# Order of the down-projection products: W11 of a round ahead of W22 of the round in front of it

## The chip, the cores and the metric

One Trainium2 chip, one core. The metric is the device time of one execution in microseconds (us), as the median of the runs.

## The reference

A trunk of two layers over x of 512 tokens by 1024 features, in float32. Layer 0 mixes the tokens with sliding-window attention, layer 1 with gated linear attention; both are followed by the same feed-forward part, and only that part is touched here:

```python
def conv_ffn(h, w_up, conv_w, conv_b, w_down):
    u = h @ w_up
    gate, up = u[..., :D_FF], u[..., D_FF:]
    gp = jnp.pad(gate, ((0, 0), (CONV_W - 1, 0), (0, 0)))
    conv = conv_b + conv_w[0] * gp[:, 0:S]
    for i in range(1, CONV_W):
        conv = conv + conv_w[i] * gp[:, i:i + S]
    return (jax.nn.silu(conv) * up) @ w_down
    ...
        x = x + conv_ffn(rmsnorm(x, ffn_norm[i]), f_w_up[i], f_conv_w[i], f_conv_b[i], f_w_down[i])
```

D_FF is 2816, and w_down is 2816 by 1024.

## The kernel before

Every float32 product is made of three products of rounded parts: high by high, low by high, high by low. ACT rounds a weight tile to its high part, DVE subtracts to get the low part, and PE multiplies three times per block of 128 rows.

**Phases.** The feed-forward part of a layer is cut along D_FF into two chunks, of 12 and 10 feature tiles. Each chunk has an up phase and then a down phase (`down_phase`), so there are four down phases in the program, called first to fourth here: the first and third work on chunk 0, with 6 pairs of feature tiles (18 matmuls in a product), the second and fourth on chunk 1, with 5 pairs (15 matmuls).

**Rounds.** A down phase has four rounds, one for each two output tiles of 128 features. The two by two blocks (pairs of feature tiles, pairs of output tiles, halves of the tokens) are multiplied in Winograd's form, with seven products in place of eight: Z1, W11, W12, Z2, Z4, Z3 and W22. The W products take plain weight quarters; the Z products take sums of quarters. n is the number of a round over the whole program, r its number in the phase, from 0 to 3; "round two" below is r = 1, "round three" r = 2, "round four" r = 3.

**PE.** `down_product` (L536) waits for the low part of the product's weights, and multiplies into one PSUM bank. There are two sets of three banks (`SETS`), used in turn by rounds. Within a round W11, Z2, Z3 and W22 share one bank: W11 is written, *taken* (added to X by DVE, straight from the bank), Z2 is accumulated on top, taken, then Z3, taken, then W22, taken. So w22(n) waits until Z3 of round n has been taken (L586). w11(n) waits for the taking of W22 two rounds before (L561). The program order of products is `down_phase` (L589 to 611); W22 of a round is multiplied in the round behind it, second in that round's row. The same order stands in the table `ROUNDS` (L73), from which `COUNT` makes the values to wait for.

**DVE.** `down_rounds` (L1564) is its order: takings (`take`, L1484, 128x256), low parts (`weight_lo`, L1456), and the sums of quarters for Z2 and Z4 (`sum_z2` L1465, `sum_z4` L1476). sum_z2 needs W11's quarter, W11's and W12's come by DMA.

**ACT.** `down_round` (L1062) is its order: high parts (`weight_hi`, L1016) of Z3, then of the next round's Z1, this round's W22, the next round's W11, Z2, W12 and Z4. In the second and fourth phase X is final behind each round, so ACT also makes the two tiles that a round has finished: `x_tile` (L968 the scaled and rounded X for the next layer, in the second phase alone; L969 the square). The first of the two waits for the taking of Z4 of the round before, and the second for that of W22 of the round before.

**SP.** `load_round` (L373) issues the loads: W22 of round n when PE is done with W22 of round n-1 (same buffer), W11 and W12 of round n+1 when PE is done with those of round n. In round two it also issues the two first halves of the Z sums of round four (`load_21`), behind the W22 load.

**POOL.** It adds the second halves of those sums by accumulating DMAs (L1962), and in the second and fourth phase it adds the squares of the X tiles one by one into SS (`sum_square`, L1948 and L1951, 128x512). Its order there is: square 0, second half of Z1, square 1, second half of Z3, squares 2 to 5.

Of the kernel before, what the change touches and what calls it, by code (L numbers as in the profile page):

```python
# [70 lines left out]

PRODUCTS = ("Z1", "W11", "W12", "Z2", "Z4", "Z3", "W22")
ROUNDS = ((("Z1", 0), ("W11", 0), ("W12", 0), ("Z2", 0), ("Z4", 0), ("Z3", 0)),  # L73
# [3 lines left out]
COUNT = {(4 * chunk + n, name): 28 * chunk + i + 1  # L77
         for chunk in range(4) for i, (name, n) in enumerate(sum(ROUNDS, ()))}
# [16 lines left out]
def trunk(nc, xT, gains, w_qkv, sinks, rel_bias, w_o, w_bin, w_ga, w_gate, b_norm, w_bo, w_up, conv_w, conv_b,  # L95
          w_down0, w_down1, onehot, ident, causal, causal_pair, out, bias_rows):
    with ExitStack() as ctx:
# [227 lines left out]
        def _(sp):  # L325
# [20 lines left out]
            def load_down(n, name):  # L346

                sp.dma_start(DRAW[name][:, 0:down_cols(n)], quarter(n, name)).then_inc(plain[name], 16)
# [24 lines left out]
            def load_round(n, src, next_unit):  # L373

                r = n % 4
                if r:
                    sp.wait_ge(down_done, COUNT[n - 1, "W22"])
                    load_down(n, "W22")
                if r == 1:
                    layer, chunk = n // 8, n // 4 % 2  # L380
                    sp.wait_ge(al_last, 2 * layer + chunk + 1)
                    load_21(n + 2, "Z1")
                    load_21(n + 2, "Z3")
                if r < 3:
                    sp.wait_ge(down_done, COUNT[n, "W11"])
                    load_down(n + 1, "W11")
                    sp.wait_ge(down_done, COUNT[n, "W12"])
                    load_down(n + 1, "W12")
                if src is not None and r == 2:
                    sp.wait_ge(down_lo["Z3"], n)  # L390
                    load(next_unit, src[0])
                    sp.wait_ge(down_lo["Z3"], n + 1)
                    load(next_unit + 1, src[1])
# [79 lines left out]
        def _(pe):  # L473
# [76 lines left out]
            def z1(n, ready=None):  # L550
                if n % 4 == 0:
                    pe.wait_ge(unit_done, chunk_end(n))
                if n % 4 == 1:
                    pe.wait_ge(value_ready, gated_end(n) - 1)
                if n % 4 >= 2:
                    pe.wait_ge(x_taken, COUNT[n - 2, "Z4"])
                down_product(n, "Z1", SETS[n % 2][2], True, ready)

            def w11(n, ready=None):
                if n % 4 >= 2:  # L560
                    pe.wait_ge(x_taken, COUNT[n - 2, "W22"])  # L561
                down_product(n, "W11", SETS[n % 2][0], True, ready)
# [22 lines left out]
            def w22(n):  # L585
                pe.wait_ge(x_taken, COUNT[n, "Z3"])  # L586
                down_product(n, "W22", SETS[n % 2][0], False)

            def down_phase(layer, chunk):  # L589
                n = 8 * layer + 4 * chunk  # L590
                parts = AL_LAYER * layer + AL_COUNT[chunk]
                z1(n, lambda kb: parts + 2 * kb + 1)
                w11(n)
                w12(n, lambda kb: parts + 2 * kb + 2)
                z2(n, lambda kb: parts + 2 * kb + 2 + (kb == PAIRS[chunk] - 1))
                z4(n)
                z3(n)
                for m in (n + 1, n + 2):
                    z1(m)
                    w22(m - 1)  # L600
                    w11(m)
                    w12(m)
                    z2(m)
                    z4(m)
                    z3(m)
                w11(n + 3)
                w22(n + 2)
                z1(n + 3)
                z2(n + 3)
                z4(n + 3)  # L610
                z3(n + 3)
                w12(n + 3)
# [726 lines left out]
        def _(dve):  # L1339
# [148 lines left out]
            def take_w11(n):  # L1488
                take(n, "W11", 0, 0, t1, ALU.add)
# [16 lines left out]
            def take_w22(n):  # L1506
                take(n, "W22", 0, 1, t1, ALU.subtract)
# [56 lines left out]
            def down_rounds(n, st, next_unit):  # L1564

                take_z1(n)
                last_lo(n // 8, n // 4 % 2, PAIRS[n // 4 % 2] - 1, 5, 7)
                weight_lo(n, "Z4")
                weight_lo(n, "Z3")
                take_w12(n)  # L1570
                take_z2(n)
                sum_z2(n + 1)
                weight_lo(n + 1, "Z1")
                take_z4(n)
                weight_lo(n, "W22")
                weight_lo(n + 1, "W11")
                sum_z4(n + 1)
                for m in (n + 1, n + 2):
                    take_z3(m - 1)
                    weight_lo(m, "W12")  # L1580
                    weight_lo(m, "Z2")
                    take_z1(m)
                    weight_lo(m, "Z4")
                    take_w22(m - 1)
                    weight_lo(m, "Z3")
                    take_w11(m)
                    take_w12(m)
                    weight_lo(m, "W22")
                    take_z2(m)
                    sum_z2(m + 1)  # L1590
                    if m == n + 1:
                        weight_lo(m + 1, "Z1")
                        take_z4(m)
                        sum_z4(m + 1)
                        weight_lo(m + 1, "W11")
                    else:
                        weight_lo(m + 1, "W11")
                        take_z4(m)
                        sum_z4(m + 1)
                        weight_lo(m + 1, "Z1")  # L1600
                m = n + 3
                take_z3(m - 1)
                weight_lo(m, "Z2")
                take_w11(m)
                weight_lo(m, "Z4")
                take_w22(m - 1)
                weight_lo(m, "W12")
                weight_lo(m, "Z3")
                if st is not None:
                    x_lo(st, 0)  # L1610
                take_z1(m)
                if st is not None:
                    x_lo(st, 1)
                    x_lo(st, 2)
                take_z2(m)
                weight_lo(m, "W22")
                if st is not None:
                    x_lo(st, 3)
                take_z4(m)
                if next_unit is not None:  # L1620
                    lo_unit(next_unit)
                if st is not None:
                    x_lo(st, 4)
                take_z3(m)
                if st is not None:
                    x_lo(st, 5)
                if next_unit is not None:
                    lo_unit(next_unit + 1)
# [513 lines left out]
```

## Time and profile before

| what | value |
|---|---|
| time, median of 3 runs | 1089.37 us (1086.51 to 1090.02) |
| time of the profiled execution | 1087.98 us |
| its span, first to last instruction | 1086.2 us |
| mean granted TensorE clock | 0.996 |
| PE busy | 1072.6 us, 99% |
| DVE busy | 752.9 us, 69% |
| ACT busy | 493.5 us, 45% |
| POOL busy | 117.3 us, 11% |
| DMA, mean rate | 112 GB/s |

Busy time is the time in which the profiler shows an instruction on an engine. PE's matmuls overlap in the record, so a busy PE can still have small delays between the starts of its matmuls; these are found from the number of matmuls in a stretch and the stretch's length. PEld is the weight load of PE, which runs ahead of its matmul.

### The profile page before, as it was taken

What the parts mean: (1) busy time and instruction counts of PE and PEld (TensorE: products, weight loads), DVE (VectorE), ACT (ScalarE), POOL (GpSimd) and SP (SyncE); (2) the same over time, 40 slices, a digit from 0 to 9 for tenths busy, and PEclk for the clock granted to TensorE, in tenths of its full rate; (3) what the DMA queues carried; (4) which work ended last, traced back from release to release, by engine and by line L of the source; (5) the groups of instructions that cost most, each with busy time, mean ns of one, the idle gap of its engine ahead of it and who ended that gap; (6) DMA issues with size and microseconds to landing.
All of it is one profiled execution on the core that took longest, in us unless ns stands there. A gap on an engine that the chain in (4) does not pass through costs nothing.

```text
span 1086.2 us, 15688 instructions
## 1 busy us (share of the span) xinstructions
PE 1072.6 (99%) x5920; PEld 921.5 (85%) x5920; DVE 752.9 (69%) x1098; ACT 493.5 (45%) x766; POOL 117.3 (11%) x109
## 2 busy tenths in 40 slices
PE   9999999999999999999999999999999999999996
PEld 7888788888899888898888888788888899888896
DVE  6588667676876667787544566867676876667786
ACT  7366554343533334454652335454344432344452
POOL 3100030000100000123021221130000100000122
PEclk9999999999999999999999999999999999999998
DMA  7511032225652225552222211232226652225542
GB/s 211 168 59 59 27 110 97 97 97 183 161 161 98 96 95 170 135 161 71 78 78 97 78 44 56 72 108 92 96 96 184 159 172 87 97 97 169 133 122 91
DMA packets 43804, 121.12 MB, mean 112 GB/s; under 512 B 5250, under 2 KB 10530, under 8 KB 43748
## 3 DMA queue, kind: packets, MB, share of 16 engines
q1 hardware_dynamic: 36308, 106.81, 28.9%
q0 software_dynamic: 4608, 11.54, 6.5%
q10 hardware_dynamic: 2832, 2.01, 1.1%
q8 instruction: 37, 0.61, 0.2%
q14 instruction: 19, 0.16, 0.0%
HBM read 116.93 MB, written 2.88 MB: 110 GB/s over the span
## 4 chain that ended last, share of the span: by engine, by line
PE 94%; DVE 3%; ACT 1%; DMA 1%; issue 0%; SPq 0%; DVEq 0%
PE PS L486 68%; PE PS L544 19%; PE PS L666 1%; PE PS L684 1%; PE PS L674 1%; DVE XL L1368 1%; DMA X<-xT 1%; PE PS L816 1%; DVE X L1916 1%; PE PS L848 0%; PE PS L835 0%; PE PS L819 0%; PE PS L850 0%; PE PS L745 0%; PE PS L772 0%
## 5 line engine op out<-in xcount | busy, mean ns | idle before, releaser
L486 PE MATMUL PS<-XH,WH 128*128 128x512 f32 x992 | 391.4, 395 | 1.0 <-DVE WL L1663 1.0
L486 PE MATMUL PS<-XH,WL 128*128 128x512 f32 x992 | 386.4, 389 | 0.0
L486 PE MATMUL PS<-XL,WH 128*128 128x512 f32 x992 | 386.1, 389 | 0.0
L486 PEld LDWEIGHTS PS<-XH,WH 128*128 128x128 f32 x992 | 186.2, 188 | 42.1 <-issue 2.1
L486 PEld LDWEIGHTS PS<-XH,WL 128*128 128x128 f32 x992 | 186.2, 188 | 39.4
L486 PEld LDWEIGHTS PS<-XL,WH 128*128 128x128 f32 x992 | 186.3, 188 | 38.4 <-issue 1.0
L939 ACT CAST WH<-WRAW 128x1024 fp32r<-128x1024 f32 x134 | 139.5, 1045 | 161.1 <-DMA WRAW<-w_up 110.3
L1351 DVE TENSOR_TENSOR WL<-WRAW,WH 128x1024 fp32r<-128x1024 f32 x134 | 168.6, 1258 | 16.2 <-ACT WH L939 15.7
L1389 DVE TENSOR_TENSOR GS<-PS,R 128x512 f32<-128x512 f32 x44 | 30.4, 692 | 118.8 <-PE PS L486 118.8
L544 PE MATMUL PS<-AH,DH_Z 128*128 128x256 f32 x352 | 98.2, 279 | 0.3
L544 PE MATMUL PS<-AH,DL_Z 128*128 128x256 f32 x352 | 97.6, 277 | 0.0
L544 PE MATMUL PS<-AL,DH_Z 128*128 128x256 f32 x352 | 97.6, 277 | 0.0
L982 ACT ACTIVATE CV<-GS,CONVB,CONVW 128x512 f32<-128x512 f32 x44 | 36.0, 819 | 89.0 <-DVE GS L1389 89.0
L544 PE MATMUL PS<-AH,DH_W 128*128 128x256 f32 x264 | 73.7, 279 | 0.2 <-DVE X L1484 0.2
L544 PE MATMUL PS<-AL,DH_W 128*128 128x256 f32 x264 | 73.2, 277 | 0.0
L544 PE MATMUL PS<-AH,DL_W 128*128 128x256 f32 x264 | 73.2, 277 | 0.0
L1484 DVE TENSOR_TENSOR X<-X,PS 128x256 f32<-128x256 f32 x112 | 46.1, 417 | 38.1 <-PE PS L544 37.7
L544 PEld LDWEIGHTS PS<-AH,DH_Z 128*128 128x128 f32 x352 | 66.4, 189 | 2.3 <-PE PS L486 1.9
L544 PEld LDWEIGHTS PS<-AL,DH_Z 128*128 128x128 f32 x352 | 66.1, 188 | 0.0
L544 PEld LDWEIGHTS PS<-AH,DL_Z 128*128 128x128 f32 x352 | 66.1, 188 | 0.0
L1016 ACT CAST DH_W<-DRAW_W 128x768 fp32r<-128x768 f32 (+1 forms) x48 | 37.0, 780 | 53.8 <-DMA DRAW_W<-w_down 53.7
L544 PEld LDWEIGHTS PS<-AH,DH_W 128*128 128x128 f32 x264 | 49.9, 189 | 0.6 <-DVE X L1484 0.6
(234 smaller groups left out, 1514.5 us busy)
## 6 DMA issues: line engine op xcount, KB each, us to landing
WRAW<-w_up SPq DMA_DIRECT2D x88, 512.0 KB, 3.3
WRAW<-w_bin SPq DMA_DIRECT2D x24, 512.0 KB, 3.3
DRAW_W<-w_down SPq DMA_DIRECT2D x24, 384.0 KB, 3.8
DRAW_W<-w_down SPq DMA_DIRECT2D x24, 320.0 KB, 3.0
WSUM_Z<-w_down SPq DMA_DIRECT2D x12, 384.0 KB, 4.8
WSUM_Z<-w_down POOLq DMA_DIRECT2D x12, 384.0 KB, 6.3
WRAW<-w_qkv SPq DMA_DIRECT2D x8, 512.0 KB, 3.4
WSUM_Z<-w_down SPq DMA_DIRECT2D x12, 320.0 KB, 3.8
```

What stands on the lines that cost most here:

```text
L486: last = mm(PS[:, bank], w[:, c:c + P], x[:, kb], start=start and n == 0 and w is wh and x is hi, stop=stop and n == len(kbs) - 1 and w is wl)
L544: last = mm(PS[:, bank, 0:TH], w[:, c], act_part[:, kb, x], start=start and kb == 0 and w is DH[name] and act_part is AH, stop=kb == PAIRS ...
L666: last = mm(PS[:, B4 + k % 2, c:c + P], q, keys[:, first:first + P], start=True, stop=True)
L674: last = nc.tensor.transpose(PS[:, B6, i * P:(i + 1) * P], PB[:, k % 2, i], IDENT[:])
L684: last = mm(PS[64 * half:64 * half + 64, B7, j * P:(j + 1) * P], V[:, 1 - j if p else 0, p, g * HD:(g + 1) * HD], PT[:, k % 2, 2 * j + hal ...
L816: mm(PS[:, B4, c], EN[:, h, c], EP[:, h, c], start=True, stop=True)
L939: nc.scalar.copy(WH[s][:], WRAW[s][:]).then_inc(hi_ready, 1)
L982: A(CV[:, par], GS[:, par, 2:T + 2], ACT.Identity, bias=CONVB[:, layer, tile], scale=CONVW[:, layer, tile, 2]).then_inc(c0_ready, 1)
L1016: nc.scalar.copy(DH[name][:, c], raw[:, c]).then_inc(down_hi[name], 1)
L1351: tt(WL[s][:], WRAW[s][:], WH[s][:].bitcast(F32), ALU.subtract).then_inc(lo_ready, 1)
L1389: tt(GS[:, par, 2:T + 2], PS[:, 2 * par], R[:], ALU.mult).then_inc(unit_evac, 2)
L1484: tt(x, x, PS[:, SETS[n % 2][bank], 0:TH], op).then_inc(x_taken, 1)
```

## The change

In rounds two and three of each down phase, W11 of the round is multiplied ahead of W22 of the round before. The takings on DVE follow this order, and so do the waits and loads on SP: in these rounds the wait for W11 and the load of the next W11 stand first, then the wait for W22 and its load, then the two `load_21` of round two, then W12. Nothing is added or taken away. ACT and POOL keep their orders.

```diff
@@ ROUNDS
-          (("Z1", 1), ("W22", 0), ("W11", 1), ("W12", 1), ("Z2", 1), ("Z4", 1), ("Z3", 1)),
-          (("Z1", 2), ("W22", 1), ("W11", 2), ("W12", 2), ("Z2", 2), ("Z4", 2), ("Z3", 2)),
+          (("Z1", 1), ("W11", 1), ("W22", 0), ("W12", 1), ("Z2", 1), ("Z4", 1), ("Z3", 1)),
+          (("Z1", 2), ("W11", 2), ("W22", 1), ("W12", 2), ("Z2", 2), ("Z4", 2), ("Z3", 2)),
@@ load_round (SP)
                 r = n % 4
+                if r in (1, 2):
+                    sp.wait_ge(down_done, COUNT[n, "W11"])
+                    load_down(n + 1, "W11")
                 if r:
                     sp.wait_ge(down_done, COUNT[n - 1, "W22"])
                     load_down(n, "W22")
...
-                if r < 3:
+                if r == 0:
                     sp.wait_ge(down_done, COUNT[n, "W11"])
                     load_down(n + 1, "W11")
+                if r < 3:
                     sp.wait_ge(down_done, COUNT[n, "W12"])
                     load_down(n + 1, "W12")
@@ down_phase (PE)
                     z1(m)
+                    w11(m)
                     w22(m - 1)
-                    w11(m)
                     w12(m)
@@ down_rounds (DVE)
                     take_z1(m)
                     weight_lo(m, "Z4")
+                    take_w11(m)
+                    weight_lo(m, "Z3")
                     take_w22(m - 1)
-                    weight_lo(m, "Z3")
-                    take_w11(m)
                     take_w12(m)
```

On PE, at the start of round two of the first phase (the names end in the product: DH_ and DL_ are the high and low parts of its weights), before:

```order
L544 MATMUL PS<-AH_117,DH_Z1_72 128x256
L544 MATMUL PS<-AL_118,DH_Z1_72 128x256
L544 MATMUL PS<-AH_117,DL_Z1_73 128x256
L544 MATMUL PS<-AH_117,DH_W22_69 128x256
L544 MATMUL PS<-AL_118,DH_W22_69 128x256
L544 MATMUL PS<-AH_117,DL_W22_70 128x256
```

and now:

```order
L548 MATMUL PS<-AH_117,DH_Z1_72 128x256
L548 MATMUL PS<-AL_118,DH_Z1_72 128x256
L548 MATMUL PS<-AH_117,DL_Z1_73 128x256
L548 MATMUL PS<-AH_117,DH_W11_75 128x256
L548 MATMUL PS<-AL_118,DH_W11_75 128x256
L548 MATMUL PS<-AH_117,DL_W11_76 128x256
```

Behind Z1 now comes W11, and W22 follows where W11 stood.

On SP, the loads of rounds two and three of the first phase (DRAW_ is the buffer that a quarter lands in, WSUM_Z13 and WSUM_Z33 those of `load_21`; the name in brackets is the semaphore waited for), before:

```order
L348 DMA DRAW_W22_71<-w_down0 128x768 [waits down_done]
L352 DMA WSUM_Z13_126<-w_down0 128x768 [waits al_last]
L352 DMA WSUM_Z33_125<-w_down0 128x768
L348 DMA DRAW_W11_77<-w_down0 128x768 [waits down_done]
L348 DMA DRAW_W12_83<-w_down0 128x768 [waits down_done]
L348 DMA DRAW_W22_71<-w_down0 128x768 [waits down_done]
L348 DMA DRAW_W11_77<-w_down0 128x768 [waits down_done]
L348 DMA DRAW_W12_83<-w_down0 128x768 [waits down_done]
```

and now:

```order
L348 DMA DRAW_W11_77<-w_down0 128x768 [waits down_done]
L348 DMA DRAW_W22_71<-w_down0 128x768 [waits down_done]
L352 DMA WSUM_Z13_126<-w_down0 128x768 [waits al_last]
L352 DMA WSUM_Z33_125<-w_down0 128x768
L348 DMA DRAW_W12_83<-w_down0 128x768 [waits down_done]
L348 DMA DRAW_W11_77<-w_down0 128x768 [waits down_done]
L348 DMA DRAW_W22_71<-w_down0 128x768 [waits down_done]
L348 DMA DRAW_W12_83<-w_down0 128x768 [waits down_done]
```

The load of W11 has moved in front of that of W22 and of the two `load_21`. DVE's two takings that change places read alike in such a list (both are X from PS), and the low part of Z3 stays between them.

## Rows read from the trace of the kernel before

**Rows 1.** The page, busy time of each engine over the span.
```profile
PE 1072.6 (99%) x5920; PEld 921.5 (85%) x5920; DVE 752.9 (69%) x1098; ACT 493.5 (45%) x766; POOL 117.3 (11%) x109
```

**Rows 2.** Windows, PE's down matmuls in the four phases: length, busy (count), clock, DMA.
```profile
287.38:344.63 57.25, 57.25 (x504) 1.00 0.47 134
453.66:503.44 49.78, 49.56 (x420) 1.00 0.45 129
856.92:914.16 57.24, 57.24 (x504) 1.00 0.46 133
1023.20:1070.81 47.61, 47.56 (x405) 1.00 0.40 104
```

**Rows 3.** Windows, PE's down matmuls over five products at two places.
```profile
455.49:463.99 8.50, 8.50 (x78) 1.00 0.32 103
...
479.90:488.73 8.83, 8.83 (x78) 1.00 0.68 232
```

**Rows 4.** Timeline, PE's weight loads: start, us, engine, line, operands [idle before <-releaser].
```profile
465.66 0.19 PEld L544 LDWEIGHTS PS<-AH,DH_W 128*128 128x128 f32 x1
...
1047.31 0.19 PEld L544 LDWEIGHTS PS<-AH,DL_Z 128*128 128x128 f32 x1
1047.74 0.19 PEld L544 LDWEIGHTS PS<-AH,DH_W 128*128 128x128 f32 x1 [0.24 <-DVE X L1484]
```

**Rows 5.** Timeline, DVE in the second down phase.
```profile
462.98 1.56 DVE L1456 TENSOR_TENSOR DL_W<-DRAW_W,DH_W 128x640 fp32r<-128x640 f32 x2
...
465.19 0.42 DVE L1484 TENSOR_TENSOR X<-X,PS 128x256 f32<-128x256 f32 x1
...
469.52 0.41 DVE L1484 TENSOR_TENSOR X<-X,PS 128x256 f32<-128x256 f32 x1
...
474.12 0.83 DVE L1465 TENSOR_TENSOR DRAW_Z<-WSUM_Z,DRAW_W 128x640 f32<-128x640 f32 x1 [0.67 <-DMA DRAW_W<-w_down]
...
476.67 0.82 DVE L1456 TENSOR_TENSOR DL_W<-DRAW_W,DH_W 128x640 fp32r<-128x640 f32 x1
...
479.53 1.58 DVE L1456 TENSOR_TENSOR DL_Z<-DRAW_Z,DH_Z 128x640 fp32r<-128x640 f32 x1
...
485.40 0.42 DVE L1484 TENSOR_TENSOR X<-X,PS 128x256 f32<-128x256 f32 x1 [0.55 <-PE PS L544]
```

**Rows 6.** Timeline, ACT in round two of the second phase.
```profile
468.90 0.72 ACT L968 ACTIVATE XH<-X,GAIN 128x512 fp32r<-128x512 f32 x1 [1.10 <-DVE X L1484]
...
470.05 0.71 ACT L1016 CAST DH_Z<-WSUM_Z 128x640 fp32r<-128x640 f32 x1
470.67 0.72 ACT L1016 CAST DH_W<-DRAW_W 128x640 fp32r<-128x640 f32 x1
```

**Rows 7.** Timeline, SP: issue of W22's and the next W11's load, second phase.
```profile
467.72 0.33 SPq L348 DMA_DIRECT2D DRAW_W<-w_down  x1
...
469.49 0.33 SPq L348 DMA_DIRECT2D DRAW_W<-w_down  x1
```

**Rows 8.** DMA issues: W22's load in round two, phases first to fourth; last number: landing.
```profile
DRAW_W<-w_down SPq DMA_DIRECT2D x1, 384.0 KB, 4.2
...
DRAW_W<-w_down SPq DMA_DIRECT2D x1, 320.0 KB, 2.7
...
DRAW_W<-w_down SPq DMA_DIRECT2D x1, 384.0 KB, 3.0
...
DRAW_W<-w_down SPq DMA_DIRECT2D x1, 320.0 KB, 3.2
```

**Rows 9.** Timeline, POOL's additions of squares, rounds two and four of the second phase.
```profile
472.50 1.62 POOL L1951 TENSOR_TENSOR SS<-SS,SQ 128x512 f32<-128x512 f32 x1
...
490.41 1.29 POOL L1951 TENSOR_TENSOR SS<-SS,SQ 128x512 f32<-128x512 f32 x1 [6.24 <-ACT SQ L969]
```

**Rows 10.** Timeline, DVE in round two of the fourth phase.
```profile
1042.96 1.85 DVE L1465 TENSOR_TENSOR DRAW_Z<-WSUM_Z,DRAW_W 128x640 f32<-128x640 f32 x1 [0.22 <-DMA DRAW_W<-w_down]
```

**Rows 11.** Windows, DVE in round four of the second phase.
```profile
492.46:502.25 9.79, 9.79 (x16) 1.00 0.25 85
```

## The prediction

> **What bounds the kernel now.** The page first: PE is busy for 99% of the span [rows 1], so what can be won lies in the small delays between its matmuls. I read those from the windows over PE's matmuls in the four down phases. In the first and third, 504 matmuls take 57.25 and 57.24 us, one every 0.1136 us [rows 2], with no wait that I could find: this is PE's own pace, and nothing can be won there. At this pace the 420 matmuls of the second phase would take 47.71 us and the 405 of the fourth (its last product left out) 46.01; they take 49.78 and 47.61 [rows 2]. **2.07 and 1.60 us, 3.67 together (0.34%), is all that any order of these products can give back.**
>
> Two things make up this loss. One is plain waits. W22's first weight load in round two of the second phase starts at 465.66; it was due about 0.08 earlier, and the taking of Z3 that it needs ended at 465.19 + 0.42 = 465.61 [rows 4, 5]. In round three of the fourth phase the same load starts 0.43 us behind its predecessor in place of 0.12, released by a taking: 0.31 lost [rows 4]. The other is pace: five products (75 matmuls; the windows also count those that reach over an edge) take 8.50 us before the first stall and 8.83 after it, at the same granted clock of 1.00 [rows 3]. So after a stall a matmul starts every 0.1177 us in place of 0.1133, and the trace of the second phase goes on so for some 18 products: 15 x 18 x 0.0044 = 1.2 us.
>
> **The change, part by part**, worked out for the second phase, since its rows are the fullest. A product is 15 x 0.1133 = 1.70 us. Round two's Z1 starts at 463.99 (the end of the first window of [rows 3]) in both kernels.
>
> *W11 moved ahead of W22.* W11 is now due at 463.99 + 1.70 = 465.69. Its low part is ready at 462.98 + 1.56 = 464.54 [rows 5]: no wait. W22 is due at 467.39, and Z3 was taken at 465.61: the wait of 0.08 is gone, and PE keeps its fast pace. In round three W11 comes 1.7 us earlier than now, so its low part is the new thing that can be late (below).
>
> *SP.* A load is issued 0.19 behind its product's end (W22 ends at 467.53, issue at 467.72 [rows 7]). W11's next load goes out at 467.39 + 0.19 = 467.58, and no longer at 469.49 [rows 7]; DVE's sum for Z2, which waited 0.67 us for it [rows 5], finds it landed. W22's load goes from 467.72 to 469.09 + 0.19 = 469.28, and the two load_21 behind it from about 468.1 to 469.7.
>
> *ACT and DVE behind W22's load.* It lands after 2.7 us [rows 8], at 472.0. ACT has by then taken the second X tile (it waits for the taking of W22, which now stands where W11's stood, 469.52 + 0.41 = 469.93 [rows 5]; 1.15 for the tile and 0.62 for Z1's high part [rows 6] make 471.7), so the DMA sets the time: high part 472.0 to 472.8 (0.73), low part to 473.6, then the taking of Z2, 473.55 + 0.42 = 474.0. Z3 is due at 463.99 + 6 x 1.70 = 474.19. So PE isn't held as long as the load lands within 2.9 us; with W22's 18 matmuls and 768 columns the same sum in the first and third phase gives 3.7 us. The rows say 4.2, 2.7, 3.0 and 3.2 for the four phases [rows 8]: **the first exceeds its bound by 0.5, the fourth by 0.3.** sum_z2 starts at 473.9 in place of 474.12 [rows 5]: DVE's late start and the earlier W11 cancel.
>
> *POOL.* Its addition of square 1 stands behind the second half of Z1 that follows load_21. In the trace it runs at 472.50 for 1.62 us [rows 9], when DVE mostly waits. It now comes some 1.6 us later, 474.1 to 475.7, on top of DVE's unbroken run of sum, low part of Z1, taking, sum, low part of W11. What this costs DVE I take from ops that met such an addition: 1.58 us in place of 0.82 [rows 5] and 1.85 in place of 0.83 [rows 10], 0.76 to 1.02; nothing if it meets a wait of DVE. I take 0.76, the second phase's own. Low part of W11, by starts 0.735 apart, a taking 0.335: 473.9 + 0.735 + 0.735 + 0.335 + 0.735 + 0.82 = 477.26, + 0.76 = 478.0. PE wants it at 463.99 + 8 x 1.70 = 477.59. **PE waits 0.4 at W11 of round three**, and the slow pace starts there. At the product behind (W12 of round three, now at 481.66) PE is then at 477.59 + 0.4 + 0.08 + 2 x 1.77 = 481.6. The gain of the first step is given back.
>
> *Round three to the end, second phase.* W22's load moves by 1.7 us again: issued about 481.8, landed 484.6, low part done at 486.2, so Z2's taking starts at 486.2 and no longer at 485.40 [rows 5]: 0.8 late. DVE then works without a gap into round four, where the addition of square 4 (490.41 [rows 9]) comes as much later and holds a low part again. From 492.46 to 502.25 DVE has no idle time at all, 9.79 of 9.79 us busy [rows 11], and PE's last products wait for its takings: the lateness goes through whole. Bounds: 0 (if round three's slack takes it) and 1.7 (the whole shift). I take **+0.9**, near the 0.8 just worked out.
>
> *Fourth phase.* No rounded X tile, so ACT is freer. Z3 of round two waits 0.3 (above), W11 of round three about 0.5, and the old losses there, 0.31 and a stall before it, go: **+0.3**, between -1.6 (its whole loss) and +2.
>
> *First and third.* DVE has gaps there and POOL adds no squares. The third's load lands in time: 0. The first's, if it lands in 4.2 us again, stalls Z3 by 0.5, and the slow pace holds for the 15 products behind, 270 x 0.0044 = 1.2: +1.7. If it lands within 3.7, nothing. I take half, **+0.85**.
>
> A fit in the Trainium skill, "DMA: Bandwidth & Descriptors", in "Anatomy of one DMA" (2.0 us and the bytes over 436 GB/s, made for transfers that GpSimd issues), gives 2.9 us for such a load as an estimate. By it the first phase costs nothing and the sum would be +1.2. The row of 4.2 speaks against it here, that of 3.0 for it.
>
> Sum: +0.9 + 0.3 + 0.85 = +2.05. The profiled execution took 1087.98 us, of which 1086.2 are the span and 1.8 lie around it; it would take 1090.0. It stands 1.39 below the median of 1089.37, so the median becomes **1091.4 us**. A change under 0.3%, 3.3 us, can't be told from none here.
>
> **The rivals.**
> - *The load is hidden everywhere* (all of W22's loads land within their bounds). For it: two of four rows. Then only the second phase's late DVE and a little of the fourth are left: +1.2, 1090.6.
> - *A gain.* POOL's addition falls into a wait of DVE, or DVE's ops keep it out. The Trainium skill, "SBUF — State Buffer", in "SBUF: two separate sides", says that VectorE and GpSimd share a port pair as an exclusive lock, held for a whole instruction by whichever starts first. Ops back to back would then delay POOL and not DVE until a taking lets it in. Then W11's low part is ready at 477.26, before 477.59, PE keeps its pace, and the 1.2 us of slow pace and 0.08 of the second phase and 0.7 of the fourth return: -2.0, 1087.4. Against it: the op of 1.58 us in the same phase, and DVE's full round four. The faster side needs nearly all of the 3.67.
> - *W22's load becomes the bound* (the side of slower). From 2.9 us on in the second and fourth phase, and 3.7 in the first and third, Z3 waits in round two and again in round three. If all land in 4.2 us: 1.3 at the first and about 0.6 at the second, +1.9 in each of second and fourth, +1.7 in each of first and third: +7.2, 1096.6. With landings between, +3.3 to +5. For it: the row of 4.2, and that the load now starts while W11's is still landing.
> - *It doesn't matter* (the new waits are as long as the old): 1089.4.
>
> **How the numbers follow.** Forecast 0.42 (0.02 of it over the bound of slower), hidden load 0.15, gain 0.14 (0.04 of it faster by over 0.3%), W22's load as the bound 0.24, no effect 0.05. So faster 0.04, same 0.70, slower 0.26. The range goes from 1087.8, just above the gain, to 1095.0, which takes in most of the load's case; about 0.1 is left out on each side.
>
> **What would show it.** Right: no wait of PE at W22 in rounds two and three; in the second and fourth phase a wait at W11 of round three released by its low part, or at Z3 by the taking of Z2; W22's load issued some 1.6 us later; POOL's addition of square 1 over a sum or low part of DVE that takes 1.6 us or more; the second phase longer than 49.78 us. Wrong: the second phase at 48.5 us or less, or the first and third both over 58 us (then the load's price was set too low).

## The result, and the profile after

The changed kernel takes 1091.36 us in the median of 11 runs (1090.09 to 1092.12), the kernel before, beside it on the same chip, 1088.4 us in the median of 11 (1086.51 to 1090.02). The ratio is 1.0025, with a 95% interval of 1.0015 to 1.0034: slower by 3.0 us, which is real, and less than 0.3%. The time forecast was 1091.4. That it fits so well is partly luck: the forecast added 2.05 us to a median of three runs, 1089.37, that stood 1.0 us above the median of eleven, and the true step was 2.96.

The profiled execution took 1092.12 us with a span of 1090.2, 4.0 more than before. The page, busy time (before: [rows 1]):

```profile
PE 1071.8 (98%) x5920; PEld 920.0 (84%) x5920; DVE 755.1 (69%) x1098; ACT 492.4 (45%) x766; POOL 117.7 (11%) x109
```

DVE is busy for 2.2 us more, with the same 1098 instructions: something stretches them. The windows over PE's down matmuls in the four phases (length, busy, count, clock, DMA):

```profile
288.26:345.61 57.35, 57.35 (x504) 1.00 0.43 130
454.65:506.34 51.69, 49.22 (x420) 1.00 0.44 126
859.83:917.07 57.24, 57.24 (x504) 1.00 0.44 132
1026.11:1074.80 48.69, 47.42 (x405) 1.00 0.36 98
```

Beside [rows 2]: +0.10, +1.91, 0.00 and +1.08, together 3.09. The clock is the same. The rest of the span's 4.0 is the 0.88 by which the first down phase starts later, ahead of any product that was moved; the medians' difference, 2.96, is near the 3.09 without it. So 2.99 of the loss is in the second and fourth phase. PE's waits (line, releaser: total, times, longest), in 453 to 507 us,

```profile
PE PS L548 <- DVE DL_Z L1460: 1.3, 1, 1.3
PE PS L548 <- DVE X L1488: 1.0, 1, 1.0
```

and in 1026 to 1075 us:

```profile
PE PS L548 <- DVE DL_Z L1460: 1.3, 1, 1.3
```

The first and third of these are one wait: **Z1 of round three, for its low part**. By the starts of the matmuls it costs 1.56 us in the second phase and 1.51 in the fourth (the profile's 1.3 counts only from the modelled end of the matmul before). It was not there before (0.00 and 0.26). The second is Z4 of round four, 1.29, also new. DVE in the second phase, and below it the same sum in the fourth:

```profile
473.91 0.83 DVE L1460 TENSOR_TENSOR DL_W<-DRAW_W,DH_W 128x640 fp32r<-128x640 f32 x1 [1.51 <-ACT DH_W L1020]
474.65 0.42 DVE L1488 TENSOR_TENSOR X<-X,PS 128x256 f32<-128x256 f32 x1
474.98 2.57 DVE L1469 TENSOR_TENSOR DRAW_Z<-WSUM_Z,DRAW_W 128x640 f32<-128x640 f32 x1
477.48 0.81 DVE L1460 TENSOR_TENSOR DL_Z<-WSUM_Z,DH_Z 128x640 fp32r<-128x640 f32 x1
...
496.83 1.78 DVE L1372 SCALAR_TENSOR_TENSOR XL<-X,GAIN,XH 128x512 fp32r<-128x512 f32 x1
...
1046.57 2.51 DVE L1469 TENSOR_TENSOR DRAW_Z<-WSUM_Z,DRAW_W 128x640 f32<-128x640 f32 x1
```

The third row is the sum for Z2, 0.83 us before [rows 5], now 2.57. POOL at the same times:

```profile
474.68 0.86 POOL L1966 DMA_DIRECT2D WSUM_Z<-w_down  x1 [5.84 <-DMA WSUM_Z<-w_down]
475.25 1.61 POOL L1955 TENSOR_TENSOR SS<-SS,SQ 128x512 f32<-128x512 f32 x1
...
496.46 1.60 POOL L1955 TENSOR_TENSOR SS<-SS,SQ 128x512 f32<-128x512 f32 x1 [0.97 <-ACT SQ L973]
...
1046.74 1.64 POOL L1955 TENSOR_TENSOR SS<-SS,SQ 128x512 f32<-128x512 f32 x1
```

POOL's addition ends at 475.25 + 1.61 = 476.86, DVE's sum at 477.55, 0.69 behind it. In the fourth phase 1048.38 and 1049.08: 0.70. The sum is nearly all done after the addition; then comes the low part of Z1 (477.48 to 478.29), and PE takes it up at once (Z1 starts at 478.43; it was due at 476.87). The landings of W22's load in round two (last number), first to fourth phase:

```profile
DRAW_W<-w_down SPq DMA_DIRECT2D x1, 384.0 KB, 3.7
...
DRAW_W<-w_down SPq DMA_DIRECT2D x1, 320.0 KB, 2.9
...
DRAW_W<-w_down SPq DMA_DIRECT2D x1, 384.0 KB, 3.1
...
DRAW_W<-w_down SPq DMA_DIRECT2D x1, 320.0 KB, 3.0
```

The first, second and fourth are on the bound that the prediction set (3.7 and 2.9) within 0.1, the third is 0.6 inside it, and Z3 of round two waits 0.08, 0.06, 0.00 and 0.18 us.

**Theory A**, for the experiments: the load is late by one product (1.7 us), with it the loads of the halves behind it, POOL and DVE's sum; so POOL's addition of square 1 falls on the sum and holds it to its own end. **Theory B**: W22's load is the cost, DVE waits for its high part and everything behind is late. **Theory C**: the new order of the products and takings costs by itself, in either round.

### The profile page after: what moved, and what is told of

Its sections match the earlier page's. It is cut to its first block, busy times and chain, and to the rows that moved or that the text cites. A ratio compares the mean times of both kernels' runs of the same rounds, so it can differ in the third digit from the quotient of the medians.

```text
span 1090.2 us, 15688 instructions
## 1 busy us (share of the span) xinstructions
PE 1071.8 (98%) x5920; PEld 920.0 (84%) x5920; DVE 755.1 (69%) x1098; ACT 492.4 (45%) x766; POOL 117.7 (11%) x109
## 4 chain that ended last, share of the span: by engine, by line
PE 93%; DVE 4%; DMA 1%; ACT 1%; issue 1%; SPq 0%; DVEq 0%
PE PS L490 68%; PE PS L548 18%; PE PS L670 1%; DMA DRAW_W<-w_down 1%; PE PS L688 1%; PE PS L678 1%; DMA X<-xT 1%; DVE XL L1372 1%; PE PS L820 1%; DVE X L1920 1%; PE PS L852 0%; PE PS L839 0%; PE PS L823 0%; PE PS L854 0%; PE PS L749 0%
## 5 line engine op out<-in xcount | busy, mean ns | idle before, releaser
L1460 DVE TENSOR_TENSOR DL_W<-DRAW_W,DH_W 128x768 fp32r<-128x768 f32 (+1 forms) x48 | 42.6, 896 | 12.7 <-ACT DH_W L1020 12.7
```

What stands on the lines that cost most here:

```text
L1460: tt(DL[name][:, c], raw[:, c], DH[name][:, c].bitcast(F32), ALU.subtract).then_inc(down_lo[name], 1)
```

## The experiments

A wait at a product is the extra time before its first and its second matmul together, by starts of matmuls; phase lengths are those of the windows. Experiments 1 to 4 ran on one chip and 5 to 12 on another, each beside the kernel before.

**1 and 2. The swap in one round alone.** Table, product order, takings and loads go back to the order before in the other round. Against the changed kernel, experiment 1 (swap in round two alone) and then 2 (in round three alone):

```diff
-          (("Z1", 2), ("W11", 2), ("W22", 1), ("W12", 2), ("Z2", 2), ("Z4", 2), ("Z3", 2)),
+          (("Z1", 2), ("W22", 1), ("W11", 2), ("W12", 2), ("Z2", 2), ("Z4", 2), ("Z3", 2)),
...
-                if r in (1, 2):
+                if r == 1:
```

```diff
-          (("Z1", 1), ("W11", 1), ("W22", 0), ("W12", 1), ("Z2", 1), ("Z4", 1), ("Z3", 1)),
+          (("Z1", 1), ("W22", 0), ("W11", 1), ("W12", 1), ("Z2", 1), ("Z4", 1), ("Z3", 1)),
...
-                if r in (1, 2):
+                if r == 2:
```

> The change in round two alone; round three as before. Both theories: round two's wait comes back (1.5 us at Z1 of round three in the second and fourth phase), since W22's load of round two is late and the two load_21 with it. If round two carries it all, the second phase is 51 to 52 us and the fourth 48.4 to 48.9; if round three carries half, the second is about 50.7.

> The change in round three alone; round two as before. If round two carries the loss (theory P in its narrow form), the fourth phase stays at 47.6 and the second is at 49.8 to 50.6: what is left is W22's load of round three, issued 1.7 us later, which makes DVE's taking of Z2 some 0.8 us late there. If the lateness of W22's load is what counts, round three loses as much as round two: the second phase is at 50.7 or more.

Round two alone: median 1090.37, ratio 1.0019 (1.0010 to 1.0029); phases 57.25, 51.44, 57.25, 47.94, with Z1 of round three waiting 1.57 and 1.53. Round three alone: 1089.01, ratio 1.0007 (0.9998 to 1.0017); phases 57.25, 50.33, 57.40, 46.52, and Z1 of round three waits 0.25 and 0.00. The long wait belongs to the swap in round two, where the load of the halves and POOL's addition of square 1 stand behind W22's load. Theory C fails for round three: there the swap costs 0.55 in the second phase (Z4 of round four waits 1.05) and gives 1.09 back in the fourth, where no change was expected. Some 0.7 of this 1.09 is pace, since 30 matmuls run at the slow one in place of 194; in experiment 1 too the fourth phase came out shorter than expected, at the fast pace nearly throughout. The waits are the surer reading.

**3 and 4. POOL's addition of square 1 ahead of the second half of Z1**, in the changed kernel and in the kernel before:

```diff
+                    if chunk:
+                        sum_square(st + 1, 1)
                     add_quarter(n + 3, "Z1")
-                    if chunk:
-                        sum_square(st + 1, 1)
                     add_quarter(n + 3, "Z3")
```

> The changed kernel, with POOL's addition of square 1 ahead of the second half of Z1 (in the second and fourth phase). Theory P (the addition of square 1, behind the accumulating DMA, falls on DVE's sum for Z2 and holds it, 2.57 us in place of 0.83): the addition now runs at about 472.7 in the second phase, while DVE waits for W22's high part; the sum takes 0.83 us again, the wait of 1.5 us at Z1 of round three goes from both phases, the second phase takes 50.0 to 50.7 us (51.69 now) and the fourth, without its last product, 47.2 us (48.69); the time is 1088.5. Theory L (W22's load, issued 1.7 us later, is the bound by itself): the sum still ends too late, Z1 of round three still waits for over 1 us, and both phases stay within 0.4 us of 51.69 and 48.69.

> The kernel before, with the same move on POOL. Theory P: the additions no longer meet the sum of the fourth phase (1.85 us there), the waits of 0.3 at Z1 and at W22 of round three go; the fourth phase takes 46.2 to 47.2 us in place of 47.61, the second stays at 49.8 within 0.5; 1087.5 in all. Theory L: nothing changes by more than 0.3 us in either phase.

Changed kernel: 1088.39, ratio to before 1.0001 (0.9992 to 1.0010), phases 57.24, 50.02, 57.24, 46.96. Kernel before: 1088.03, ratio 1.0001 (0.9992 to 1.0010), 57.25, 49.80, 57.25, 47.44. One line moved on POOL takes the loss away, and does not change the time of the kernel before. There its fourth phase had been expected at 47.2 or less: the waits of 0.3 at Z1 and W22 of round three did go, but 299 matmuls ran at the slow pace in place of 194, and took 0.5 back. DVE's sum in the changed kernel with this edit, second phase,

```profile
473.98 0.82 DVE L1469 TENSOR_TENSOR DRAW_Z<-WSUM_Z,DRAW_W 128x640 f32<-128x640 f32 x1
```

and POOL's addition, now in a wait of DVE:

```profile
471.17 1.29 POOL L1955 TENSOR_TENSOR SS<-SS,SQ 128x512 f32<-128x512 f32 x1 [3.50 <-ACT SQ L973]
```

The wait at Z1 of round three is gone in both phases. W22's load is as late as in the changed kernel, so theory B has little left: Z3 of round two waits 0.23 and 0.33.

**5. The changed kernel without W22's loads of rounds two and three.** W22's parts are then made from what lies in its buffer as soon as PE is done with it, so the output is not the reference's. The line that drops the loads:

```diff
-                    load_down(n, "W22")
+                    if r == 3:
+                        load_down(n, "W22")
```

> The changed kernel without W22's loads in rounds two and three: ACT rounds what lies in the buffer as soon as PE is done with it, so the output is another and only the 2.9 us of the transfer are gone from the chain. Theory P+L (W22's late load pushes DVE's sum for Z2 into the time when POOL is about to add square 1): in the second phase ACT is busy until 472.7 of the trace of the change, so W22's low part comes 0.45 us earlier, the sum starts just ahead of POOL's addition and the low part of Z1 behind it is held instead: Z1 of round three still waits 0.3 to 1 us. In the fourth phase, where ACT is free 1.3 us earlier, the sum is done ahead of the addition; the wait at Z1 goes below 0.3 us and the phase, without its last product, takes 46.3 to 47 us (48.69 now). Theory P alone (the addition costs the same wherever the sum starts): both waits at Z1 stay within 0.2 of 1.5 us.

One run, 1091.2; phases 57.24, 51.23, 57.24, 47.84. Z1 of round three still waits, 1.28 and 0.86, and the sum still takes 2.63 us, beside an addition at 475.34. Neither outcome as written: the waits are shorter than 1.5, and the fourth phase isn't near 47. Taking the transfer away gives 0.46 and 0.85 of 1.91 and 1.08. But this edit moves the addition as well. Counted from the starts of the phases (455.11 and 1026.08) it ends 0.37 and 0.84 us earlier than in the changed kernel, and the waits at Z3 and Z1 together are shorter by 0.35 and 0.83. So PE's loss follows the addition's end, and the transfer acts by where it puts the addition.

**6 and 7. POOL's additions cut to 4 of 512 columns in the second and fourth phase, in the changed kernel and in the kernel before**, which leaves out nearly all of these sums of squares:

```diff
+                w = 4 if st in (2, 4) else T
...
-                    nc.gpsimd.tensor_tensor(SS[:], SS[:], SQ[:, par], ALU.add).then_inc(ss_ready, 1)
+                    nc.gpsimd.tensor_tensor(SS[:, 0:w], SS[:, 0:w], SQ[:, par, 0:w], ALU.add).then_inc(ss_ready, 1)
```

> The changed kernel with POOL's additions of the squares made over 4 columns in place of 512 in the second and fourth phase (the sum of squares that the output needs is not computed there). Theory P: no DVE op is held for over 1 us in these phases; the waits at Z1 of round three (1.56 and 1.51) and at Z4 of round four (1.29) fall to under 0.2 each; the second phase takes 48.3 to 49.5 us and the fourth 46.3 to 46.9. Theory L: the late load remains, Z1 of round three waits over 1 us, and the second phase stays above 51 us.

> The kernel before, with the POOL engine's additions of squares cut to 4 of 512 columns in the second and fourth phase (so part of the sums of squares is left out, and the output is not the reference's). The counterpart of e6_small_squares, for what the additions cost before. If the changed kernel was hurt because its order moved the addition onto DVE's sum, the additions cost the kernel before much less than the 3.3 and 1.6 us that they cost the changed one: about 1 us in the second phase (48.8), and 0.3 in the fourth (47.3). If they cost as much here, the collision was there all along and the swap is not what made it matter: 46.5 and 46.

One run each, 1087.7 and 1086.4. The second and fourth phase of the kernel before, without the additions:

```profile
454.08:503.27 49.19, 49.19 (x420) 1.00 0.50 136
1023.02:1069.14 46.12, 46.12 (x405) 1.00 0.40 104
```

The changed kernel has 48.36 and 47.05. The additions thus cost the kernel before 0.6 and 1.5 us, and the changed one 3.3 and 1.6. Over both phases: with additions the change costs 100.38 - 97.39 = 2.99, without them 95.41 - 95.31 = 0.10. **Without the additions the two kernels take the same time in these executions.** This is a balance, though, and not the absence of a cost. The changed order is 0.93 longer in the fourth phase, with Z3 waiting 0.46 and 0.35, and faster by 0.83 in the second, where the kernel before runs 313 matmuls at the slow pace, 1.4 us worth, and the changed one none. With each slow matmul taken off at 0.0044 us, the swap costs 1.5 us over both phases without the additions and 4.2 with them. Nor does the fourth phase split as expected: the additions cost 1.5 us there before (expected 0.3), as much as after. Each is one run; the firmer proof that the additions carry the net loss is experiments 3 and 4, with 11 runs each. DVE and POOL in the changed kernel without additions:

```profile
475.09 0.82 DVE L1469 TENSOR_TENSOR DRAW_Z<-WSUM_Z,DRAW_W 128x640 f32<-128x640 f32 x1
```

```profile
474.88 0.86 POOL L1967 DMA_DIRECT2D WSUM_Z<-w_down  x1 [5.85 <-DMA WSUM_Z<-w_down]
475.45 0.53 POOL L1956 TENSOR_TENSOR SS<-SS,SQ 128x4 f32<-128x4 f32 x1
```

The accumulating DMA's 0.86 us on POOL lies over the sum and does not hold it.

**8. The loads of the halves ahead of W22's load**, so that POOL is as early as before and W22's load meets more traffic:

```diff
-                if r:
-                    sp.wait_ge(down_done, COUNT[n - 1, "W22"])
-                    load_down(n, "W22")
                 if r == 1:
...
                     load_21(n + 2, "Z1")
                     load_21(n + 2, "Z3")
+                if r:
+                    sp.wait_ge(down_done, COUNT[n - 1, "W22"])
+                    load_down(n, "W22")
```

> The changed kernel, with the loads of the two halves of Z1 and Z3 of round four issued ahead of W22's load in round two (they wait for less). The POOL engine's DMA and its addition of square 1 then come about as early as in the kernel before, and W22's load lands later by the bytes ahead of it, 0.5 to 1 us. If the loss comes from the addition meeting DVE's sum for Z2, the wait at Z1 of round three goes down from 1.5 to 0.5 us or less, and the second phase is near 50.5. If the loss comes from W22's load being late, the wait stays at 1.5 us or grows, and PE may wait at Z3 of round two also: 52 us or more.

1093.87, ratio 1.0055 (1.0040 to 1.0071), the slowest of all; phases 58.77, 51.42, 58.27, 47.92. Neither outcome as written: both parts came true. The collision is gone, and the load is late. DVE, second phase:

```profile
476.41 0.83 DVE L1460 TENSOR_TENSOR DL_W<-DRAW_W,DH_W 128x640 fp32r<-128x640 f32 x1 [3.03 <-ACT DH_W L1020]
...
477.48 0.82 DVE L1469 TENSOR_TENSOR DRAW_Z<-WSUM_Z,DRAW_W 128x640 f32<-128x640 f32 x1
```

POOL's addition (474.53 to 476.14) falls into DVE's wait of 3.03 us; the sum takes 0.82, and Z1 of round three doesn't wait. But W22's load, issued at the same point of the phase (15.61 us behind its start, in both kernels), lands after

```profile
DRAW_W<-w_down SPq DMA_DIRECT2D x1, 320.0 KB, 4.4
```

in place of 2.9, and Z3 of round two waits 1.56 us: the excess over the bound of 2.9, 1.5, goes straight to PE. The first and third phase lose 1.52 and 1.01 in the same way; there too the load is issued at the same point as in the changed kernel (18.67 and 18.68 us behind the starts), and lands after

```profile
DRAW_W<-w_down SPq DMA_DIRECT2D x1, 384.0 KB, 5.1
...
DRAW_W<-w_down SPq DMA_DIRECT2D x1, 384.0 KB, 4.6
```

against the bound of 3.7.

**9 and 12. Mending the order.** The changed kernel with POOL's addition first, and with W22's low part moved behind the sum for Z4 (in round two also behind W11's low part), so that DVE doesn't wait for W22's high part ahead of the taking of Z2 (W22 is not needed before two more products, now that W11 stands ahead of it):

```diff
                     take_w12(m)
-                    weight_lo(m, "W22")
                     take_z2(m)
...
                         sum_z4(m + 1)
                         weight_lo(m + 1, "W11")
+                        weight_lo(m, "W22")
...
                         sum_z4(m + 1)
+                        weight_lo(m, "W22")
                         weight_lo(m + 1, "Z1")
```

> The changed kernel with square 1 first on POOL and, on DVE, W22's low part moved behind the next round's W11 (round two) or the sum for Z4 (round three), where nothing waits for it yet. If W22's load acts through DVE's order alone (DVE waits for its high part and the taking of Z2 stands behind it), the waits of PE at Z3 of rounds two and three (0.23 and 0.14 in the second phase, 0.33 in the fourth, of the kernel with square 1 first) go; the second phase falls from 50.02 to about 49.6, the fourth from 46.96 to 46.1 to 46.6. If the load acts otherwise, nothing changes by over 0.2 us.

> The kernel of e9_low_later once more, beside e11_low_later_before on the same chip: 1087.2, phases of 57.2, 49.2, 57.2 and 46.4. If its lead over the kernel before (0.8 us) was chance, it comes out within 0.2 us of it.

1087.21, ratio 0.9990 (0.9981 to 0.9999), then 1087.0, ratio 0.9993 (0.9984 to 1.0002). This is the best version found, 0.8 to 0.9 us under the kernel before in both comparisons: under 0.3%, and at the edge of what its runs can tell from none. The windows of the second execution:

```profile
287.92:345.17 57.25, 57.25 (x504) 1.00 0.48 132
454.20:503.68 49.48, 48.83 (x420) 1.00 0.50 134
857.15:914.40 57.25, 57.25 (x504) 1.00 0.47 133
1023.43:1069.49 46.06, 46.06 (x405) 1.00 0.41 106
```

The fourth phase stands at its floor of 46.01 (in the first execution it was 46.44, with 89 matmuls at the slow pace); what the second still loses lies in round four.

**10. The taking of Z1 ahead of X's first low part in round four**, added to 9, against the wait at Z4 of round four. In the changed kernel that was 1.29 us, behind the X tile (496.83, 1.78 us) that POOL's addition holds; in experiment 9 it had already come down to 0.26:

```diff
+                take_z1(m)
                 if st is not None:
                     x_lo(st, 0)
-                take_z1(m)
-                if st is not None:
                     x_lo(st, 1)
```

> As e9_low_later, and in round four of the second phase DVE takes Z1 ahead of the first low part of the next layer's X, which a POOL addition holds for 1.77 us. The wait of PE at Z4 of round four (1.29) falls to under 0.3 us; DVE has no idle time from there to the phase's end, so W22 of round four may wait longer in turn: the second phase 48.7 to 49.6 us, the fourth as in e9. In all 1086.5 to 1087.5, the first version below the kernel before.

1087.4, ratio 0.9992 (0.9983 to 1.0001); second phase 49.81. Z4 no longer waits, but W22 of round three (in round four) waits 0.60 and Z3 1.01, in place of 0.00 and 0.64 (0.35 and 0.66 in the second execution of that kernel): the lateness moves to the next product. No gain.

**11. The mends of 9 in the kernel before**, where W22's low part stands ahead of W11's, since W22 is multiplied first. Round two's part of the edit, to which POOL's line and round three's are added as in 9:

```diff
+                        weight_lo(m, "W22")
                         weight_lo(m + 1, "W11")
```

> The kernel before with the two mends of e9_low_later: the addition of square 1 ahead of the second half of Z1, and the low part of W22 taken out of its place ahead of the taking of Z2 and put behind the sum for Z4. In this order W22 still comes ahead of W11, so its low part stands ahead of W11's. If what e9 won comes from these mends alone, and the order of W11 and W22 does not matter once they are in, this kernel comes out like e9: second phase 49.2, fourth 46.4, median 1087.2 beside 1088.0 of the kernel before. If W22 behind Z1 is really too early for its parts (the order's own worth), the low part moved back makes the wait at W22 of round three longer than its 0.3, the second phase stays at 49.8 or goes over 50, and the median stays at 1088 or more.

1089.59, ratio 1.0013 (1.0004 to 1.0022), 2.6 us above 12 on the same chip; phases 58.34, 49.49, 57.25, 46.97. In the first phase W22 waits 1.08 us in round three. DVE's sum for Z2 there, in this kernel,

```profile
312.96 0.96 DVE L1465 TENSOR_TENSOR DRAW_Z<-WSUM_Z,DRAW_W 128x768 f32<-128x768 f32 x1 [1.32 <-DMA DRAW_W<-w_down]
```

and in that of 12:

```profile
311.03 0.95 DVE L1469 TENSOR_TENSOR DRAW_Z<-WSUM_Z,DRAW_W 128x768 f32<-128x768 f32 x1
```

From the starts of the phases (288.45 and 287.92) that is 24.5 and 23.1 us. In the old order the sum waits for W11's load, and W22's low part now stands behind it, close to its due time; with W11 multiplied first its load goes out a product earlier and W22 is due a product later. So the later place of W22's low part needs the changed order of products: the first and fourth phase differ by 1.09 and 0.91 us between 11 and 12, the second by 0.01. What 9 gives takes both.

## Why the prediction was right, and where it was not

**The chain up to the collision was right to 0.2 us.** The second phase starts 0.99 us later in the profile after (454.65, before 453.66), so 0.99 is added to the times of the prediction:

| step, second phase | predicted | measured |
|---|---|---|
| W22's load issued | 470.27 | 470.26 |
| it lands | 472.99 | 473.12 |
| taking of Z2 starts | 474.54 | 474.65 |
| sum for Z2 starts | 474.89 | 474.98 |
| POOL's addition of square 1 starts | 475.09 | 475.25 |
| low part of Z1 starts | 475.63 | **477.48** |

**The step that failed is the price of the addition.** "I take 0.76, the second phase's own", from two ops that had met an addition, with 0.76 to 1.02 as bounds. It was 2.57 - 0.82 = 1.75, outside the bounds. The bounds were durations of two encounters, where the two ends should have been compared: in [rows 5] the op of 1.58 us ends at 479.53 + 1.58 = 481.11, and POOL's addition that it met ran 478.75 to 480.44. It too ended 0.67 behind the addition. A held op of DVE ends some 0.7 us behind the addition, so its price is what is left of the addition when it would start, and not a fixed 0.76.

**Which op is held.** The traces have two kinds of meeting, and the forecast took the price of one for the other. In the usual kind the addition comes while DVE is at work on a low part; this one runs on as if alone, and the next is held. DVE and then POOL in the profile after, a little behind the collision:

```profile
481.08 0.81 DVE L1460 TENSOR_TENSOR DL_Z<-DRAW_Z,DH_Z 128x640 fp32r<-128x640 f32 x1
481.81 0.41 DVE L1488 TENSOR_TENSOR X<-X,PS 128x256 f32<-128x256 f32 x1
482.14 1.58 DVE L1460 TENSOR_TENSOR DL_Z<-DRAW_Z,DH_Z 128x640 fp32r<-128x640 f32 x1
```

```profile
481.35 1.68 POOL L1955 TENSOR_TENSOR SS<-SS,SQ 128x512 f32<-128x512 f32 x1 [3.20 <-ACT SQ L973]
```

This costs 0.76 with a taking between the two ops, and 1.09 without (1.91 in place of 0.82, at 1048.34 before and 1052.60 after). In the other kind the op at work is held as well, from its very start: so it went with the sum for Z2, 0.27 and 0.17 us old when the addition started. By the usual kind the sum would have ended at 475.80, the addition 1.15 later and Z1's low part 0.68 behind it, at 477.63 in place of 478.29: a wait of 0.9 at Z1, as an estimate from these rows. The other 0.66 comes from the sum being held.

**So the wait's place was wrong too.** With the 0.76 at the low part of W11 PE was to wait 0.4 there. The 1.75 fell on the sum, one op ahead of Z1's low part, which had 0.2 us to spare: 1.56 at Z1 of round three. The wait at W11 behind it is 0.08.

**The terms.** Second phase +0.9, measured +1.91; fourth +0.3, measured +1.08; first +0.85, measured +0.10; third 0, measured 0. Two terms too small by 1.8 and one too large by 0.75 gave +2.05 for 3.09. The bounds of the fourth, -1.6 to +2, held; those of the second, 0 to 1.7, did not.

**The first phase.** The load landed in 3.7 us and not in 4.2, so half of a 1.7 us loss was not due: 0.08 of waiting, and no slow pace behind it. The bound itself was right; experiment 8 crossed that of 2.9 by 1.5 and PE waited 1.56.

**Pace.** "The slow pace starts there" was wrong for the second phase. PE's matmuls from W22 of round three on, two products behind the long stall, in four products of the second phase and five of the fourth:

```profile
482.04:488.84 6.80, 6.80 (x62) 1.00 0.64 207
```

```profile
1053.60:1062.43 8.83, 8.83 (x77) 1.00 0.35 111
```

6.80 is 4 x 1.70, the fast pace, and 8.83 is the slow one of [rows 3]. In the second phase 18 matmuls ran at the slow pace after the change and 271 before, so 253 x 0.0044 = 1.1 us were won back there by pace; without this the phase would have cost 3.0. The prediction had counted this gain as given back at W11.

**The two waits removed** (W22 in rounds two and three) are gone, as forecast. **Late DVE into round four** was there, but as a new wait at Z4 (1.29): X's low part took 1.78 us, held by square 5's addition, ending at 498.61 behind POOL's 498.06, with the taking of Z1 behind it. That POOL's ops come later and hold an op again was in the prediction; only its size was not.

**The rivals.** *W22's load as the bound* did not happen here (0.00 to 0.18 us of waiting), but was near: experiment 8 made it so, 1093.87. *A gain* was to come if the addition fell into a wait of DVE: experiments 3 and 9 put it there, and their medians are 3.0 and 4.2 us under that of the change. Against the kernel before that is no difference and 0.8 us, not the 2.0 of this rival. As for the rule named with it (the Trainium skill, "SBUF — State Buffer", "SBUF: two separate sides"), by which whoever starts first holds the lock for a whole instruction: the traces agree that a whole instruction is waited out, and mostly on who waits. In the second and fourth phase, over the twelve traces with whole additions, a low part (of a weight or of X) was at work 56 times when an addition started, and took 0.74 to 0.82 us each time, as if alone; the addition ended 1.14 us or more behind it. In six more meetings the sum for Z2 was the older by 0.17 to 0.43 us and was held all the same (the profile after and experiments 1 and 5, two each). In these six the addition stands right behind POOL's own DMA, whose record (0.86 to 0.88 us) reaches 0.3 into that of the addition. Why they differ stays open: in experiment 6 the same DMA and an addition of 4 columns did not hold the sum, and POOL's starts are rough.

## What to carry over

When an instruction moves, find what moves with it on queues behind it (here a load took two other loads and so POOL's DMA and addition along), and ask what each of them now lies on top of. An op of VectorE that an addition of GpSimd holds costs what is left of that addition, so read such a price from the two ends, not from the op's length; look which of two neighbouring ops is the held one, and put the addition where VectorE waits anyway. And when a product is made due later, its preparation has to be moved back as well, or it holds up what has become more urgent: here the new order and the new place of its preparation each lost time without the other, and together came out level with the kernel before or a little ahead (0.8 to 0.9 us).

## What the runs showed of the hardware that I had not expected

- **A DVE op with both inputs in SBUF doesn't share with a POOL addition.** A held one ended 0.67 to 0.70 us behind the addition's end (481.11 behind 480.44 before; 477.55 behind 476.86 and 1049.08 behind 1048.38 after; 477.64 behind 476.95 in experiment 5); an X tile's low part ended 0.55 behind (498.61 and 498.06). It is mutual: an addition that found such an op at work took 1.48 to 2.43 us, and 1.28 to 1.30 alone. Right behind POOL's own DMA it took 1.61 to 1.65, also where it met no such op at work (474.53 in experiment 8).
- **Takings, which read PSUM and X, are not held.** Those that lie wholly inside an addition, 69 in the second and fourth phases of these twelve traces, took 0.40 to 0.42 us, as elsewhere.
- **A stall draws the pace.** A matmul starts every 0.1133 or 0.1177 us, at the granted clock of 1.00, and the pace changes only at a stall: after stalls of 1.5 us both were seen (8.50 us for five products in experiment 8, and 8.83 above), and behind the same stall of 0.07 to 0.09 at W22 of round two of the second phase the pace was slow in the kernel before and in experiments 4 and 7 (271, 273 and 313 matmuls, to the next stall or the end), fast in experiments 2 and 11. The kernel of 9 and 12 had 89 slow matmuls in the fourth phase of one execution and no such stretch in the other. What decides it stays open; it is worth up to 1.4 us in a phase, as much as the waits. Of a wait as counted here, 0.08 to 0.11 us lies between the product's first and second matmul, which start 0.19 to 0.22 us apart.
- **A load's landing depends on the loads in flight ahead of it**: in the second phase 320 KB landed in 2.9 us, and in 4.4 with two more loads of 320 KB issued 0.85 and 1.33 us ahead (experiment 8).
